# PEER's first products from slab 44 on: three 256-column products a chunk instead of one of 512 and one of 256, with no fold on VectorE

## The chip, the cores and the metric

One Trainium2 chip, one of its cores. The metric is the device time of one execution in microseconds (us), as the median of several runs. The kernel before takes 2194.0 us (three runs, 2193.04 to 2195.11).

## The reference

A small transformer over 256 tokens of width 1024, in float32: an MLA attention layer, a PEER layer, a GLA layer, a second PEER layer, and then a block with two kinds of local attention and a gated FFN. The change lies in PEER, which is run twice:

```python
def one_block(xi):
    q = (xi @ w_query).reshape(B, T, PEER_HEADS, 2, PEER_HALF)
    s = jnp.einsum('bthcd,cnd->bthcn', q, sub_keys)
    s_top, i_top = lax.top_k(s, PEER_TOPK)
    cand = s_top[..., 0, :, None] + s_top[..., 1, None, :]
    ...
    gate = jax.nn.softmax(best, axis=-1)
    u = u_tab[idx]
    h = jax.nn.gelu(jnp.einsum('bthkd,btd->bthk', u, xi), approximate=False)
    w = (gate * h)
    return jnp.einsum('bthk,bthkd->btd', w, v_tab[idx])
```

The kernel gathers nothing. It multiplies all 16384 rows of u (128 slabs of 128 experts) with all tokens, takes Gelu of everything, multiplies with a gate that is zero for the experts that were not chosen, and multiplies the result with all of v. So each PEER layer is two dense products of 256 x 1024 x 16384.

## The kernel before, in words

**Products in parts.** Every float32 weight and every activation is split into a high part (rounded to the type that TensorE multiplies in one pass, fp32r) and a low part, the rest. A product is then the sum of three: high weight x high activation, high weight x low activation, low weight x high activation.

**The slab stream.** Weights come in slabs of 128 x 1024 float32 (512 KB), in one order fixed for the whole kernel. SyncE loads slab n into `raw` (4 buffers, L237). ScalarE writes the high part `hi` (`split_hi`, L250) once the products of slab n-3 have been made (semaphore `eaten`; `hi` and `lo` have 3 buffers, `RING`). GpSimd or VectorE writes `lo` (`split_lo`, L259). TensorE waits for `hi_done`, does the products with `hi`, waits for the low part, does those with `lo`, and raises `eaten`. A slab's parts stand in buffers of 1088 columns, and the pair (a, b) at the end of `add_slab` says how many columns in the high and the low part begin: `SKEW` is 16 columns, which is 64 bytes.

**The activations** `xx` are 8 chunks (c) of 128 rows x 512 columns: 256 columns of the high part `xh`, then 256 of the low part `xl`.

**First products of PEER** (`first(i)`, i = 0 to 127, u). In slabs 0 to 43 each chunk c takes three products of 256 columns: `hi` with `xh` (L1434), `hi` with `xl` (L1435) and `lo` with `xh` (L1439), 24 a slab, all added up in the same 256 columns of bank i % 3. From slab 44 (`LEAD`) on, `hi` is the stationary operand of one product of 512 columns over `xh` and `xl` together (L1428, seven a slab, and the eighth in L1442 after the low ones), and `lo` that of one of 256 columns (L1439, eight a slab). The high-high and high-low sums then stand beside one another in the bank, and VectorE adds them up (`fold`, L1712, into `whole`) before ScalarE takes Gelu (L1562, L1564).

**What else runs from slab 44 on.** Until then VectorE finds the chosen experts. After that, in 64 of 84 slabs, a group of 4 tokens is turned into gates: VectorE writes one-hot rows (L1700, L1702, L1704), ScalarE their low parts (L1581), TensorE makes eight small f16 products behind the slab's own (`sums`, L1467), and VectorE multiplies the gates in (`gate_slab` L1720, `apply` L1728). The pattern repeats every five slabs: four with a group behind them, one without.

**Second products** (`second(v)`, v): the activations are stationary and the slab moves, twelve products of 512 columns each (L1480, L1481, L1487). They need `pe_ml`, which VectorE writes (L1734).

Every engine works through its own fixed list of instructions; nothing is reordered while the kernel runs.

Of the kernel before, what the change touches and what calls it, by code (L numbers as in the profile page):

```python
# [8 lines left out]
ALU = mybir.AluOpType  # L9
ACT = mybir.ActivationFunctionType  # L10
AX_X = mybir.AxisListType.X
# [6 lines left out]
P = 128  # L18
D = 1024
KD = D // P  # L20
T = 256
# [14 lines left out]
H_P, NK, TOPK = 8, 128, 16  # L36
# [64 lines left out]
SKEW, SLOT = 16, 1088  # L101
# [50 lines left out]
def add_slab(k, src, x, e, low, skew=(0, 0)):  # L152

    k.lows[low] += 1
    k.slabs.append((src, x, e, skew))
    k.lo_at.append((low, k.lows[low]))


def weight_stream(k):
# [16 lines left out]
    for l in range(2):  # L176
        w = k.dram[f"w_query{l}"]
        for c in range(2):
            for b in range(4):
                add_slab(k, rows_of(w, 2 * b, 2, c * 512, 512), 2, 512, k.lo_dve, (SKEW, SKEW))  # L180
        for i in range(NK):
            add_slab(k, k.dram["peer_u"][l, i], KD, P, k.lo_pool, (0 if i >= LEAD else SKEW, SKEW))
        for i in range(NK):
            add_slab(k, k.dram["peer_v"][l, i].unsqueeze(1), 1, D, k.lo_dve)
        if l == 0:
            w = k.dram["gla_w_in"]
            for c0 in (G_Q, G_LOW, G_K, G_V, G_V + 512, G_R, G_R + 512):
                if c0 == G_LOW:
                    add_slab(k, rows_of(w, 0, KD, c0, R_G), KD, R_G, k.lo_dve)
                else:  # L190
                    for b in range(4):
                        add_slab(k, rows_of(w, 2 * b, 2, c0, 512), 2, 512, k.lo_dve,
                                 (SKEW, SKEW) if c0 in (G_Q, G_K) else (0, 0))
            out_slabs(k, k.dram["gla_w_o"])
# [1084 lines left out]
TURN, LEAD = 41, 44  # L1279
# [23 lines left out]
def peer(k, l, s0, norm, after):  # L1303
# [3 lines left out]
    first_part = k.sig("bd_first_part")  # L1307
    G = NT * H_P
    names = ("q_act", "q_dve", "zeroed", "keyed", "scored", "s_act", "s_dve", "counted", "raised", "powered",
             "ranked", "turned", "equal", "hotted", "lowered", "summed", "spread", "applied", "bent", "gated", "m_hi", "m_lo", "folded")  # L1310
    (q_act, q_dve, zeroed, keyed, scored, s_act, s_dve, counted, raised, powered, ranked, turned, equal, hotted,
     lowered, summed, spread, applied, bent, gated, m_hi, m_lo, folded) = (k.sig(f"pe_{x}") for x in names)
    hi, lo = k.hi, k.lo
    u0, v0, end = s0 + U0, s0 + V0, s0 + SLABS
    with ExitStack() as ctx:
        hidden = k.sb(ctx, "pe_hidden", [P, NK, T])
# [5 lines left out]
        mh = k.sb(ctx, "pe_mh", [P, 2, T], F32R)  # L1322
        ml = k.sb(ctx, "pe_ml", [P, 2, T], F32R)
        count = k.sb(ctx, "pe_count", [P, NK], I32)
        whole = k.sb(ctx, "pe_whole", [P, 2, T])

# [39 lines left out]
        with k.nc.Block() as block:  # L1368
# [11 lines left out]
            def _(pe):  # L1380
# [33 lines left out]
                def first(i):  # L1414

                    r = (u0 + i) % RING
                    if i >= 3:

                        j = i - 3
                        if j > LEAD:  # L1420
                            pe.wait_ge(gated.sem, gated_before(j))
                        else:
                            pe.wait_ge(bent.sem, bent.at(j + 1))
                    ps = first_ps(i)
                    pe.wait_ge(k.hi_done, u0 + i + 1)
                    if i >= LEAD:
                        for c in range(KD - 1):
                            pe.matmul(k.bank[i % 3][:], hi[:, r, c * P:(c + 1) * P],  # L1428
                                      k.xx[:, c].rearrange("p s t -> p (s t)"), start=(c == 0), stop=False,
                                      skip_group_check=True)  # L1430
                    else:
                        for c in range(KD):
                            cols = slice(SKEW + c * P, SKEW + (c + 1) * P)
                            pe.matmul(ps, hi[:, r, cols], k.xh[:, c], start=(c == 0), stop=False)  # L1434
                            pe.matmul(ps, hi[:, r, cols], k.xl[:, c], start=False, stop=False)  # L1435
                    pe.wait_ge(*k.lo_at[u0 + i])
                    for c in range(KD):
                        cols = slice(SKEW + c * P, SKEW + (c + 1) * P)
                        last = pe.matmul(ps, lo[:, r, cols], k.xh[:, c], start=False,  # L1439
                                         stop=(c == KD - 1 and i < LEAD), skip_group_check=(i >= LEAD))  # L1440
                    if i >= LEAD:
                        last = pe.matmul(k.bank[i % 3][:], hi[:, r, (KD - 1) * P:KD * P],  # L1442
                                         k.xx[:, KD - 1].rearrange("p s t -> p (s t)"), start=False, stop=True,
                                         skip_group_check=True)
                    last.then_inc(k.eaten, 1)

                def turn_slots():
# [91 lines left out]
            def _(act):  # L1539
# [12 lines left out]
                def bend(i):  # L1552

                    g = grouped(i)
                    if i >= LEAD:
                        act.wait_ge(folded.sem, folded.at(i - LEAD + 1))
                    else:
                        act.wait_ge(k.eaten, u0 + i + 1)
                    ps, cut = first_ps(i), g * GROUP
                    made = whole[:, i % 2] if i >= LEAD else ps  # L1560
                    if cut:
                        last = act.activation(ps[:, 0:cut], made[:, 0:cut], ACT.Gelu)  # L1562
                    if cut < T:
                        last = act.activation(hidden[:, i, cut:], made[:, cut:], ACT.Gelu)  # L1564
                    last.then_inc(bent.sem, 1)

                def keep_sums(g):
# [30 lines left out]
                for n in range(SLABS):  # L1598
# [13 lines left out]
                    i = n - U0  # L1612
# [19 lines left out]
            def _(dve):  # L1632
# [71 lines left out]
                    dve.tensor_tensor(hot_h[:, g % 2], hot_ps(g)[:].rearrange("p (t i) -> p t i", t=GROUP), over(2, g),  # L1704
                                      ALU.mult).then_inc(hotted.sem, 1)

                def fold(i):

                    dve.wait_ge(k.eaten, u0 + i + 1)
                    if i >= LEAD + 2:  # L1710
                        dve.wait_ge(bent.sem, bent.at(i - 1))
                    dve.tensor_reduce(whole[:, i % 2], k.bank[i % 3][:].rearrange("p (s t) -> p t s", s=2), AX_X, ALU.add)\  # L1712
                       .then_inc(folded.sem, 1)

                def gate_slab(i):

                    cut = grouped(i) * GROUP
# [32 lines left out]
                one_hots(0)  # L1750
                one_hots(1)
                for i in range(LEAD, NK):
                    fold(i)
                    g = GROUP_AT.get(i)
                    if g is not None and g + 2 < GROUPS:
                        one_hots(g + 2)
                    if i > LEAD:
                        gate_slab(i)
                    if g is not None:
                        apply(g)  # L1760
                    if i >= NK - 3:
                        split_lo(k, dve, u0 + i + RING)
                    if i >= NK - 2:
                        split_middle(i - NK + 2)
# [14 lines left out]
    for x in (bent, m_hi, m_lo):  # L1779
        x.advance(NK)  # L1780
    gated.advance(NK - LEAD - 1)
    folded.advance(NK - LEAD)
    for x in (equal, hotted, lowered, summed, spread, applied):
        x.advance(GROUPS)
    for x in (zeroed, counted, raised, powered, ranked, turned):
# [1370 lines left out]
```

## Time and profile before

| | |
|---|---|
| median of three runs | 2194.0 us |
| span of the profiled execution, first to last instruction | 2186.9 us |
| TensorE busy | 2151.9 us (98%) |
| VectorE, ScalarE, GpSimd busy | 1561.2, 1249.5, 709.9 us |
| mean granted TensorE clock | 0.996 of full speed |
| slabs 44 to 127, layer 1 | 288.85 to 555.87 us |
| slabs 44 to 127, layer 2 | 1180.34 to about 1447.4 us |

The profile gives no time of its own for the profiled execution beside the span; the median of the runs is 7.1 us above it. Matmul records overlap (a product's record is longer than the distance to the next), so the pace of TensorE is read from the distance between starts, not from durations. A few records are missing from the trace, so counts can be a few short.

### The profile page before, as it was taken

How to read it: one execution, taken by the hardware profiler on the slowest of the kernel's cores; microseconds unless marked ns; L12 is line 12 of the kernel's file. 1: busy time of each engine (PE TensorE's matmuls, PEld its weight loads, DVE VectorE, ACT ScalarE, POOL GpSimd, SP SyncE). 2: the span in 40 equal slices, each digit the busy share in tenths (PEclk: the TensorE clock that was granted, in tenths of full speed). 3: DMA queues.
4: the chain of work that ended last, by engine and by line, in shares of the span. 5: the costliest groups of instructions: out<-in, count | busy, mean ns of one | idle time of the engine just before them, and what ended most of it. 6: DMA issues, size and time to landing. Idle time of an engine off the chain costs nothing. (4 is left out here: it accounts for less than half of the span.)

```text
span 2186.9 us, 35587 instructions
## 1 busy us (share of the span) xinstructions
PE 2151.9 (98%) x13179; PEld 1877.7 (86%) x13179; DVE 1561.2 (71%) x2946; ACT 1249.5 (57%) x2471; POOL 709.9 (32%) x346
## 2 busy tenths in 40 slices
PE   8899999999999999999999999999999999999999
PEld 8789998888888888887999888888888888897888
DVE  8658978888666666666698788866666669457776
ACT  6544577777455555564446777755555555555443
POOL 3217977777000000001698777730000005100000
PEclk9999999999999999999999999999999999999999
DMA  5244655555555555553555554556666656435554
GB/s 166 65 147 155 203 174 164 164 165 166 190 193 193 193 194 195 167 166 108 174 192 184 166 164 164 165 183 192 193 193 193 194 171 228 129 113 164 189 192 153
DMA packets 122956, 375.34 MB, mean 172 GB/s; under 512 B 13200, under 2 KB 18064, under 8 KB 122784
## 3 DMA queue, kind: packets, MB, share of 16 engines
q1 hardware_dynamic: 122496, 373.05, 52.7%
q8 instruction: 106, 1.74, 0.3%
q14 instruction: 66, 0.54, 0.1%
q10 hardware_dynamic: 288, 0.01, 0.0%
HBM read 371.96 MB, written 1.05 MB: 171 GB/s over the span
## 5 line engine op out<-in xcount | busy, mean ns | idle before, releaser
L250 ACT ACTIVATE hi<-raw 128x1024 fp32r<-128x1024 f32 (+2 forms) x705 | 738.3, 1048 | 359.9 <-PE bank L1439 109.7
L259 DVE TENSOR_TENSOR lo<-raw,hi 128x1024 fp32r<-128x1024 f32 (+2 forms) x447 | 542.1, 1216 | 263.3 <-ACT hi L250 262.8
L259 POOL TENSOR_TENSOR lo<-raw,hi 128x1024 fp32r<-128x1024 f32 x258 | 626.2, 2431 | 229.1 <-ACT hi L250 228.7
L1480 PE MATMUL bank<-hi,pe_mh 128*128 128x512 f32 x1016 | 395.7, 389 | 1.3 <-DVE pe_ml L1734 1.3
L1481 PE MATMUL bank<-hi,pe_ml 128*128 128x512 f32 x1016 | 395.3, 389 | 0.0
L1428 PE MATMUL bank<-xx,hi 128*128 128x512 f32 x1176 | 308.9, 401 | 0.0
L1593 ACT ACTIVATE pe_mh<-pe_hidden 128x256 fp32r<-128x256 f32 x256 | 106.9, 418 | 342.0 <-PE bank L1487 342.0
L342 POOL TENSOR_TENSOR rstd<-mean,minus_half 128x2 f32<-128x2 f32 x6 | 4.2, 704 | 898.9 <-DVE mean L335 898.9
L1439 PEld LDWEIGHTS bank<-xx,lo 128*128 128x128 f32 x2048 | 269.4, 188 | 13.9
L1439 PE MATMUL bank<-xx,lo 128*128 128x256 f32 x2048 | 280.5, 280 | 0.0
L1487 PE MATMUL bank<-lo,pe_mh 128*128 128x512 f32 x1016 | 271.6, 389 | 0.0
L1428 PEld LDWEIGHTS bank<-xx,hi 128*128 128x128 f32 x1176 | 211.2, 188 | 37.8
L1480 PEld LDWEIGHTS bank<-hi,pe_mh 128*128 128x128 f32 x1016 | 190.7, 188 | 42.1 <-DVE pe_ml L1734 2.6
L1487 PEld LDWEIGHTS bank<-lo,pe_mh 128*128 128x128 f32 x1016 | 190.7, 188 | 39.7
L1481 PEld LDWEIGHTS bank<-hi,pe_ml 128*128 128x128 f32 x1016 | 190.7, 188 | 39.4
L1734 DVE TENSOR_TENSOR pe_ml<-pe_hidden,pe_mh 128x256 fp32r<-128x256 f32 x256 | 108.9, 426 | 137.9 <-ACT pe_mh L1593 137.9
L1581 ACT ACTIVATE pe_hot_l<-bank,pe_slots 128x128 f16<-128x128 f32 x512 | 145.8, 369 | 80.3 <-DVE pe_hot_h L1704 80.3
L1434 PE MATMUL bank<-xx,hi 128*128 128x256 f32 x704 | 167.3, 279 | 0.0
L1435 PE MATMUL bank<-xx,hi 128*128 128x256 f32 x704 | 166.3, 278 | 0.0
L1712 DVE TENSOR_REDUCE pe_whole<-bank 128x256 f32<-128x512 f32 x168 | 116.2, 692 | 59.0 <-PE bank L1442 56.5
L1434 PEld LDWEIGHTS bank<-xx,hi 128*128 128x128 f32 x704 | 132.6, 188 | 0.1
L1435 PEld LDWEIGHTS bank<-xx,hi 128*128 128x128 f32 x704 | 132.5, 188 | 0.1
(418 smaller groups left out, 3405.5 us busy)
## 6 DMA issues: line engine op xcount, KB each, us to landing
raw<-in_peer_u SPq DMA_DIRECT2D x256, 512.0 KB, 3.3
raw<-in_peer_v SPq DMA_DIRECT2D x256, 512.0 KB, 3.5
raw<-in_w_gate_up SPq DMA_DIRECT2D x44, 512.0 KB, 3.5
raw<-in_w_in SPq DMA_DIRECT2D x34, 512.0 KB, 4.2
raw<-in_gla_w_in SPq DMA_DIRECT2D x24, 512.0 KB, 3.6
raw<-in_w_down SPq DMA_DIRECT2D x22, 512.0 KB, 3.3
raw<-in_w_query SPq DMA_DIRECT2D x16, 512.0 KB, 3.3
raw<-in_mla_w_o SPq DMA_DIRECT2D x8, 512.0 KB, 3.3
```

Of the source, the lines that this page charges most:

```text
L250: act.activation(k.hi[:, n % RING, at_hi:at_hi + x * e], k.raw[:, n % RAW, 0:x * e], ACT.Copy).then_inc(k.hi_done, 1)
L259: eng.tensor_tensor(k.lo[:, n % RING, at_lo:at_lo + x * e], k.raw[:, n % RAW, 0:x * e], k.hi[:, n % RING, at_hi:at_hi + x * e].bitcast(F32 ...
L1428: pe.matmul(k.bank[i % 3][:], hi[:, r, c * P:(c + 1) * P], k.xx[:, c].rearrange("p s t -> p (s t)"), start=(c == 0), stop=False, skip_grou ...
L1434: pe.matmul(ps, hi[:, r, cols], k.xh[:, c], start=(c == 0), stop=False)
L1435: pe.matmul(ps, hi[:, r, cols], k.xl[:, c], start=False, stop=False)
L1439: last = pe.matmul(ps, lo[:, r, cols], k.xh[:, c], start=False, stop=(c == KD - 1 and i < LEAD), skip_group_check=(i >= LEAD))
L1480: pe.matmul(second_ps(a, c), mh[:, v % 2, tok], hi[:, r, half], start=(v == 0), stop=False)
L1481: pe.matmul(second_ps(a, c), ml[:, v % 2, tok], hi[:, r, half], start=False, stop=False)
L1487: last = pe.matmul(second_ps(a, c), mh[:, v % 2, tok], lo[:, r, half], start=False, stop=(v == NK - 1))
L1581: last = act.activation(hot_l[:, g % 2, t], hot_ps(g)[:, t * NK:(t + 1) * NK], ACT.Copy, scale=slots[:, 3, c:c + 1])
L1712: dve.tensor_reduce(whole[:, i % 2], k.bank[i % 3][:].rearrange("p (s t) -> p t s", s=2), AX_X, ALU.add)\
L1734: dve.tensor_tensor(ml[:, v % 2], hidden[:, v], mh[:, v % 2].bitcast(F32), ALU.subtract)\
```

## The change

`first(i)` makes the 24 products of 256 columns in all 128 slabs. The high part stands 16 columns off in all of them, as the low part does already. All sums go into the bank's first 256 columns, ScalarE takes Gelu from there, and waits for `eaten` instead of for the fold. `fold`, its semaphore and its buffer are gone.

```diff
-            add_slab(k, k.dram["peer_u"][l, i], KD, P, k.lo_pool, (0 if i >= LEAD else SKEW, SKEW))
+            add_slab(k, k.dram["peer_u"][l, i], KD, P, k.lo_pool, (SKEW, SKEW))
...
                     pe.wait_ge(k.hi_done, u0 + i + 1)
-                    if i >= LEAD:
-                        for c in range(KD - 1):
-                            pe.matmul(k.bank[i % 3][:], hi[:, r, c * P:(c + 1) * P],
-                                      k.xx[:, c].rearrange("p s t -> p (s t)"), start=(c == 0), stop=False,
-                                      skip_group_check=True)
-                    else:
-                        for c in range(KD):
-                            cols = slice(SKEW + c * P, SKEW + (c + 1) * P)
-                            pe.matmul(ps, hi[:, r, cols], k.xh[:, c], start=(c == 0), stop=False)
-                            pe.matmul(ps, hi[:, r, cols], k.xl[:, c], start=False, stop=False)
+                    for c in range(KD):
+                        cols = slice(SKEW + c * P, SKEW + (c + 1) * P)
+                        pe.matmul(ps, hi[:, r, cols], k.xh[:, c], start=(c == 0), stop=False)
+                        pe.matmul(ps, hi[:, r, cols], k.xl[:, c], start=False, stop=False)
                     pe.wait_ge(*k.lo_at[u0 + i])
...
-                    if i >= LEAD:
-                        last = pe.matmul(k.bank[i % 3][:], hi[:, r, (KD - 1) * P:KD * P],
-                                         k.xx[:, KD - 1].rearrange("p s t -> p (s t)"), start=False, stop=True,
-                                         skip_group_check=True)
                     last.then_inc(k.eaten, 1)
...
-                    if i >= LEAD:
-                        act.wait_ge(folded.sem, folded.at(i - LEAD + 1))
-                    else:
-                        act.wait_ge(k.eaten, u0 + i + 1)
+                    act.wait_ge(k.eaten, u0 + i + 1)
                     ps, cut = first_ps(i), g * GROUP
-                    made = whole[:, i % 2] if i >= LEAD else ps
...
-                def fold(i):
-
-                    dve.wait_ge(k.eaten, u0 + i + 1)
-                    if i >= LEAD + 2:
-                        dve.wait_ge(bent.sem, bent.at(i - 1))
-                    dve.tensor_reduce(whole[:, i % 2], k.bank[i % 3][:].rearrange("p (s t) -> p t s", s=2), AX_X, ALU.add)\
-                       .then_inc(folded.sem, 1)
...
                 for i in range(LEAD, NK):
-                    fold(i)
```

TensorE (PE), before, slab 45 and the beginning of the group behind it; `bank<-xx,hi` is a product with a high part, `pe_hot` are the one-hot rows:

```order
L1428 MATMUL bank<-xx,hi 128x512 [waits hi_done,pe_bent]
L1428 MATMUL bank<-xx,hi 128x512 x6
L1439 MATMUL bank<-xx,lo 128x256 [waits lo_pool]
L1439 MATMUL bank<-xx,lo 128x256 x7
L1442 MATMUL bank<-xx,hi 128x512
L1467 MATMUL bank<-pe_hot_h,pe_hot_j 128x128 [waits pe_lowered,pe_hotted]
L1467 MATMUL bank<-pe_hot_l,pe_hot_j 128x128
```

TensorE after the change, the end of a slab's sixteen high products and the same group (the lines have moved up: L1427 and L1428 are now the two high products of 256 columns, L1432 the low one, L1455 the group's):

```order
L1427 MATMUL bank<-xx,hi 128x256
L1428 MATMUL bank<-xx,hi 128x256
L1432 MATMUL bank<-xx,lo 128x256 [waits lo_pool]
L1432 MATMUL bank<-xx,lo 128x256 x7
L1455 MATMUL bank<-pe_hot_h,pe_hot_j 128x128 [waits pe_lowered,pe_hotted]
L1455 MATMUL bank<-pe_hot_l,pe_hot_j 128x128
```

Eight products of 512 columns have become sixteen of 256, none of them behind the low ones any more; the group and all waits of TensorE stand where they stood.

VectorE (DVE), before, what it does for slab 46 up to the fold of slab 47:

```order
L1712 TENSOR_REDUCE pe_whole<-bank 128x256 [waits pe_bent,eaten]
L1700 TENSOR_TENSOR bank<-bank,pe_slots 128x512 [waits pe_summed,pe_lowered]
L1702 TENSOR_TENSOR pe_hot_j<-bank,pe_slots 128x512
L1704 TENSOR_TENSOR pe_hot_h<-bank,pe_slots 128x512 [waits pe_equal]
L1720 TENSOR_TENSOR pe_hidden<-pe_hidden,bank 128x8 [waits pe_spread,pe_bent]
L1728 SCALAR_TENSOR_TENSOR pe_hidden<-bank,pe_hidden 128x47x4 [waits pe_spread,pe_bent]
L1712 TENSOR_REDUCE pe_whole<-bank 128x256 [waits pe_bent,eaten]
```

VectorE after the change, the same slab (L1684, L1686, L1688 are the one-hot rows, L1696 and L1704 the gates):

```order
L1684 TENSOR_TENSOR bank<-bank,pe_slots 128x512 [waits pe_summed,pe_lowered]
L1686 TENSOR_TENSOR pe_hot_j<-bank,pe_slots 128x512
L1688 TENSOR_TENSOR pe_hot_h<-bank,pe_slots 128x512 [waits pe_equal]
L1696 TENSOR_TENSOR pe_hidden<-pe_hidden,bank 128x8 [waits pe_spread,pe_bent]
L1704 SCALAR_TENSOR_TENSOR pe_hidden<-bank,pe_hidden 128x47x4 [waits pe_spread,pe_bent]
```

Only the fold has gone; the rest stands in the same order.

VectorE before, where the first products end and the second begin (slabs 126 and 127; `pe_ml` is what the second products wait for):

```order
L1712 TENSOR_REDUCE pe_whole<-bank 128x256 [waits pe_bent,eaten]
L1720 TENSOR_TENSOR pe_hidden<-pe_hidden,bank 128x256 [waits pe_spread,pe_bent]
L259 TENSOR_TENSOR lo<-raw,hi 128x1024 [waits hi_done]
L1734 TENSOR_TENSOR pe_ml<-pe_hidden,pe_mh 128x256 [waits pe_m_hi]
L1712 TENSOR_REDUCE pe_whole<-bank 128x256 [waits pe_bent,eaten]
L1720 TENSOR_TENSOR pe_hidden<-pe_hidden,bank 128x256 [waits pe_spread,pe_bent]
L259 TENSOR_TENSOR lo<-raw,hi 128x1024 [waits hi_done]
L1734 TENSOR_TENSOR pe_ml<-pe_hidden,pe_mh 128x256 [waits pe_m_hi] x2
```

After the change, the same place (L1710 writes `pe_ml`):

```order
L1696 TENSOR_TENSOR pe_hidden<-pe_hidden,bank 128x256 [waits pe_spread,pe_bent]
L259 TENSOR_TENSOR lo<-raw,hi 128x1024 [waits hi_done]
L1710 TENSOR_TENSOR pe_ml<-pe_hidden,pe_mh 128x256 [waits pe_m_hi]
L1696 TENSOR_TENSOR pe_hidden<-pe_hidden,bank 128x256 [waits pe_spread,pe_bent]
L259 TENSOR_TENSOR lo<-raw,hi 128x1024 [waits hi_done]
L1710 TENSOR_TENSOR pe_ml<-pe_hidden,pe_mh 128x256 [waits pe_m_hi] x2
```

Here too only the fold of each slab has gone.

## Rows read from the trace of the kernel before

**Rows 1.** Page, part 1: engine busy us (share of span) xinstructions.

```profile
PE 2151.9 (98%) x13179; PEld 1877.7 (86%) x13179; DVE 1561.2 (71%) x2946; ACT 1249.5 (57%) x2471; POOL 709.9 (32%) x346
```

**Rows 2.** Waits, 292 to 540 us: engine line waited for: total us, times, longest.

```profile
ACT pe_hot_l L1581 <- DVE pe_hot_h L1704: 40.1, 62, 0.9
DVE pe_whole L1712 <- PE bank L1442: 24.9, 53, 1.1
ACT hi L250 <- PE bank L1442: 17.2, 15, 1.2
PEld bank L1467 <- issue: 9.9, 62, 0.2
```

**Rows 3.** Timeline, PE, slabs from 44 on: start us, us, engine line op xcount.

```profile
400.81 1.77 PE L1428 MATMUL bank<-xx,hi 128*128 128x512 f32 x7
402.41 1.11 PE L1439 MATMUL bank<-xx,lo 128*128 128x256 f32 x8
403.36 0.40 PE L1442 MATMUL bank<-xx,hi 128*128 128x512 f32 x1
403.60 0.23 PE L1467 MATMUL bank<-pe_hot_h,pe_hot_j 128*128 128x128 f16 x1
...
404.02 1.86 PE L1428 MATMUL bank<-xx,hi 128*128 128x512 f32 x7
405.72 1.09 PE L1439 MATMUL bank<-xx,lo 128*128 128x256 f32 x8
...
416.80 1.09 PE L1428 MATMUL bank<-xx,hi 128*128 128x512 f32 x4
```

**Rows 4.** Timeline, PE, low products of slabs 26 and 28.

```profile
241.02 1.07 PE L1439 MATMUL bank<-xx,lo 128*128 128x256 f32 x8
...
246.46 1.07 PE L1439 MATMUL bank<-xx,lo 128*128 128x256 f32 x8
```

**Rows 5.** Timeline, PE, low products of slabs 5 and 8.

```profile
182.35 1.11 PE L1439 MATMUL bank<-xx,lo 128*128 128x256 f32 x8
...
190.83 1.11 PE L1439 MATMUL bank<-xx,lo 128*128 128x256 f32 x8
```

**Rows 6.** Timeline, PE, second products, the last four of two slabs three apart.

```profile
599.67 1.07 PE L1487 MATMUL bank<-lo,pe_mh 128*128 128x512 f32 x4
...
607.83 1.07 PE L1487 MATMUL bank<-lo,pe_mh 128*128 128x512 f32 x4
```

**Rows 7.** Timeline, PE, slab 42, which follows on six transposes.

```profile
283.31 0.37 PE L1434 MATMUL bank<-xx,hi 128*128 128x256 f32 x1
...
285.22 1.07 PE L1439 MATMUL bank<-xx,lo 128*128 128x256 f32 x8
```

**Rows 8.** Timeline, PE, second block's low products: first and last of 15 slabs.

```profile
1870.20 1.07 PE L2432 MATMUL bank<-xx,lo 128*128 128x256 f32 x8
...
1942.75 1.10 PE L2432 MATMUL bank<-xx,lo 128*128 128x256 f32 x8
```

**Rows 9.** Page, part 5: the fold.

```profile
L1712 DVE TENSOR_REDUCE pe_whole<-bank 128x256 f32<-128x512 f32 x168 | 116.2, 692 | 59.0 <-PE bank L1442 56.5
```

**Rows 10.** Timeline, all engines, slab 127 and first two slabs of second products.

```profile
553.09 1.77 PE L1428 MATMUL bank<-xx,hi 128*128 128x512 f32 x7
553.35 1.06 ACT L250 ACTIVATE hi<-raw 128x1024 fp32r<-128x1024 f32 x1 [1.45 <-PE bank L1442]
...
554.71 0.42 DVE L1720 TENSOR_TENSOR pe_hidden<-pe_hidden,bank 128x256 f32<-128x256 f32 x1 [0.62 <-ACT bank L1562]
555.05 1.22 DVE L259 TENSOR_TENSOR lo<-raw,hi 128x1024 fp32r<-128x1024 f32 x1
...
556.18 0.42 DVE L1734 TENSOR_TENSOR pe_ml<-pe_hidden,pe_mh 128x256 fp32r<-128x256 f32 x1
556.52 0.68 DVE L1712 TENSOR_REDUCE pe_whole<-bank 128x256 f32<-128x512 f32 x1
556.66 0.19 PEld L1480 LDWEIGHTS bank<-hi,pe_mh 128*128 128x128 f32 x1 [0.95 <-DVE pe_ml L1734]
...
559.61 0.50 PE L1480 MATMUL bank<-hi,pe_mh 128*128 128x512 f32 x1
```

More of the change, by code:

```diff
@@ L1309, in peer @@
     names = ("q_act", "q_dve", "zeroed", "keyed", "scored", "s_act", "s_dve", "counted", "raised", "powered",
-             "ranked", "turned", "equal", "hotted", "lowered", "summed", "spread", "applied", "bent", "gated", "m_hi", "m_lo", "folded")
+             "ranked", "turned", "equal", "hotted", "lowered", "summed", "spread", "applied", "bent", "gated", "m_hi", "m_lo")
     (q_act, q_dve, zeroed, keyed, scored, s_act, s_dve, counted, raised, powered, ranked, turned, equal, hotted,
-     lowered, summed, spread, applied, bent, gated, m_hi, m_lo, folded) = (k.sig(f"pe_{x}") for x in names)
+     lowered, summed, spread, applied, bent, gated, m_hi, m_lo) = (k.sig(f"pe_{x}") for x in names)
     hi, lo = k.hi, k.lo
@@ L1324, in peer @@
         count = k.sb(ctx, "pe_count", [P, NK], I32)
-        whole = k.sb(ctx, "pe_whole", [P, 2, T])
         spare = Carver(hidden[:, NK // 2:, :].rearrange("p i t -> p (i t)"))
@@ L1438, in first @@
                         cols = slice(SKEW + c * P, SKEW + (c + 1) * P)
-                        last = pe.matmul(ps, lo[:, r, cols], k.xh[:, c], start=False,
-                                         stop=(c == KD - 1 and i < LEAD), skip_group_check=(i >= LEAD))
-                    if i >= LEAD:
-                        last = pe.matmul(k.bank[i % 3][:], hi[:, r, (KD - 1) * P:KD * P],
-                                         k.xx[:, KD - 1].rearrange("p s t -> p (s t)"), start=False, stop=True,
-                                         skip_group_check=True)
+                        last = pe.matmul(ps, lo[:, r, cols], k.xh[:, c], start=False, stop=(c == KD - 1))
                     last.then_inc(k.eaten, 1)
@@ L1554, in bend @@
                     g = grouped(i)
-                    if i >= LEAD:
-                        act.wait_ge(folded.sem, folded.at(i - LEAD + 1))
-                    else:
-                        act.wait_ge(k.eaten, u0 + i + 1)
+                    act.wait_ge(k.eaten, u0 + i + 1)
                     ps, cut = first_ps(i), g * GROUP
-                    made = whole[:, i % 2] if i >= LEAD else ps
                     if cut:
-                        last = act.activation(ps[:, 0:cut], made[:, 0:cut], ACT.Gelu)
+                        last = act.activation(ps[:, 0:cut], ps[:, 0:cut], ACT.Gelu)
                     if cut < T:
-                        last = act.activation(hidden[:, i, cut:], made[:, cut:], ACT.Gelu)
+                        last = act.activation(hidden[:, i, cut:], ps[:, cut:], ACT.Gelu)
                     last.then_inc(bent.sem, 1)
@@ L1781, in peer @@
     gated.advance(NK - LEAD - 1)
-    folded.advance(NK - LEAD)
     for x in (equal, hotted, lowered, summed, spread, applied):
```

## The prediction

> **What bounds the kernel now.** First the busy shares of the page: TensorE is busy for 98% of the span, the next engine for 71% [rows 1]. So the time is TensorE's, unless it waits. The waits of the stretch that the change touches (292 to 540 us, nearly all of slabs 44 to 127 of the first PEER layer) come next: VectorE, ScalarE and GpSimd wait there for TensorE or for one another, and TensorE for nobody; the one entry of its own is 9.9 us on the weight-load side in front of the groups' products, put down to issue [rows 2]. In 252 us TensorE gains nothing from any other engine being faster. What a slab costs there is the distance between the starts of its products, and that is what the timeline of TensorE is for.
>
> From the start of one slab that has no group in front of it to the next such slab, five slabs and four groups later, it is 416.80 - 400.81 = 15.99 us [rows 3]. A group takes from 403.60 to about 404.03, 0.43 us, so five slabs cost 15.99 - 4 x 0.43 = 14.27 us. The slab without a group in front: 400.81 to 403.60, 2.79 us. The other four: (14.27 - 2.79) / 4 = 2.87 us each. They are dearer by 0.08 to 0.09 us because the first product after the small f16 products starts late: the seven high products last 1.86 us against 1.77 [rows 3].
>
> **What three products of 256 columns cost.** The same 24 products are in this trace, in slabs 0 to 43, with both parts 64 bytes off. They run at two paces. Slabs 26 to 28: low products start at 241.02 and, two slabs later, at 246.46, so 2.72 us a slab, 113.3 ns a product [rows 4]. Slabs 5 to 8: 182.35 to 190.83, three slabs, 2.827 us a slab, 117.8 ns a product [rows 5]. I call them fast and slow; nothing waits in either, and eight low products last 1.07 us in the fast one and 1.10 to 1.11 in the slow one, which is how a pace is recognised at a glance. The columns, the places and the types are the same; the clock is full in both. So the operations alone do not decide the cost.
>
> Is there a fixed price for sixteen products instead of eight? The second products, twelve of 512 columns a slab, take (607.83 - 599.67) / 3 = 2.72 us [rows 6], the same as 24 of 256 columns at the fast pace [rows 4]: 226.7 ns against twice 113.3. I take zero. The Trainium skill ("TensorE: Matmul & The Clock Gate", section on the back-to-back issue gap) gives N / 2.4 + 2.5 ns a product, which speaks against this change: eight more products a slab would be 8 x 2.5 = 20 ns, over 168 slabs 3.4 us more. By these rows it isn't so: here each pace is 17/16 of the columns for both widths. The sum goes by the rows.
>
> Now the old form against the new, by slab. The first product after a group keeps its delay, for it comes from the change of kind in front of it: after the six transposes slab 42 needs 285.22 - 283.31 = 1.91 us for its sixteen high products, 16 x 0.1133 = 1.81 and 0.09 to 0.10 for the start [rows 7]. So:
> - fast: 2.72 + 0.09 = 2.81 after a group (before: 2.87, gain 0.06), 2.72 otherwise (before: 2.79, gain 0.07);
> - slow: 2.83 + 0.09 = 2.92 after a group (loss 0.05), 2.83 otherwise (loss 0.04).
>
> A layer has 64 slabs with a group behind them, so 64 that follow on one, and 20 others; the last of these doesn't count, because what comes after it waits for VectorE (below). All fast: 64 x 0.06 + 19 x 0.07 = 5.2 us gained a layer, 10.3 in both. All slow: 64 x 0.05 + 19 x 0.04 = 4.0 us lost, 7.9 in both. These are the bounds of the one term that matters.
>
> **Which value in between.** A pace, once taken, is kept while slabs follow on one another (5 to 8, 26 to 28), and it is taken anew after other products have come between. In the second block 256-column slabs of the same kind are broken up by small attention products just as these will be by groups: of 15 such slabs 7 are fast and 8 slow, and the marks alternate more than they cluster (the first is 1.07, the last 1.10) [rows 8]. Slab 42, after transposes, is fast [rows 7]. The old form itself shows a mark of the same kind: its eight low products last 1.11 us in the slab without a group and 1.09 in the one after [rows 3]. Nothing in the trace has f16 products of 128 columns directly in front of 256-column ones, so I take half of the slabs at either pace: -1.2 us over both layers, halfway between -10.3 and +7.9.
>
> The Trainium skill (same page, "Step-by-step: what each phase is for") says that TensorE has two independent read ports, and that loading the next weights doesn't steal from the running product. By that the slow pace would have no ground and all slabs would be fast. The trace has both paces; that sentence is the case for the first rival.
>
> **Edits of no cost.** The fold is 116.2 us of VectorE's time, 692 ns each [rows 9], and it is hidden: nobody on TensorE's side waits for it between the first and the last slabs [rows 2]. Without it the one-hot rows and the gates come earlier, ScalarE takes Gelu from the bank as it does in slabs 0 to 43, and these engines wait longer for TensorE instead. The bank of a slab comes free for the third slab after it, some 8 us later; a later Gelu could not be felt either. The high part at another offset costs ScalarE nothing that I can see a reason for; ScalarE waits for TensorE there anyway [rows 2]. DMA issues are the same and hang on the same low parts.
>
> **Where the fold does stand on the path: the switch to the second products.** TensorE's first one waits for `pe_ml`. That chain starts when slab 126's u part is needed no more, at 553.09: ScalarE's high part first (553.35), Gelu, then VectorE's gate 554.71, low part 555.05, `pe_ml` 556.18, and TensorE starts at 556.66, 3.57 us after 553.09 [rows 10]. The fold isn't in it: the gate waits for ScalarE, which was held by the high part [rows 10]. So this stays at 3.57 us, and a shorter slab 127 just waits longer; hence the slab that I leave out. The next one is different: after `pe_ml` comes the fold of slab 127, 556.52 for 0.68 us, and the gate, low part and second `pe_ml` behind it; the second V slab starts 559.61 - 556.66 = 2.95 us after the first, where the pace is 2.72 [rows 6, 10]. Without the fold I expect that 0.23 back, and a little behind it: 0.3 us a layer, 0.6 in all. Bounds: nothing, and 0.7 a layer.
>
> **Sum.** -1.2 - 0.6 = -1.8 us. The profiled span of 2186.9 us would become 2185.1; the median lies 7.1 us above that span, so 2192.2 us.
>
> **Rivals.**
> - *Nearly all slabs fast.* For it: slab 42 [rows 7], and slabs 26 to 28, which stay fast [rows 4]. Against it: 8 of 15 in rows 8. Gain 10.3 + 0.6: 2183.1 us.
> - *Nearly all slabs slow*, the one on the other side. The place is the first product after each group; the price is 24 x 4.5 ns = 0.11 us a slab above the fast pace. It decides from the point where more than about 85% of the slabs are slow, since at 57% the old form is reached (0.06 of 0.11). For it: slabs 5 to 8 stay slow though nothing disturbs them [rows 5]; the group repeats on a fixed beat, so all may fall the same way. Loss 7.9 - 0.6: 2201.3 us.
> - *The change takes the pressure off VectorE and that is the gain.* Then ScalarE's 40.1 us of waiting for the one-hot rows [rows 2] would have to reach TensorE. They don't; it would give the 0.6 us at the switch alone, 2193.4 us, inside the forecast.
>
> **How the numbers follow.** This kernel's runs lie within about 0.1% of one another, and 0.2% (4.4 us) is about what can be told from no change: the bounds are 2189.6 and 2198.4 us. Below the first the share of fast slabs must be over about two thirds, above the second under about one seventh. Mixed paces, the forecast, 0.39, with its own range 2189.6 to 2196; nearly all fast 0.37, because the two places closest in kind, in PEER itself and behind a short run of 128-column products, are both fast [rows 4, 7]; nearly all slow 0.24. Faster 0.37, same 0.39, slower 0.24. The range that leaves out a tenth at either side: 2183.0 to 2200.5.
>
> **What would show it.** In the profile after: the rows of eight low products, 1.07 (fast) or 1.10 to 1.11 (slow), counted over the 168 slabs, with 2.81 or 2.92 us from the first product after a group to the next group; 2.72 or 2.83 in the slabs without; a mixture of both is my forecast, one alone a rival. The first second product 3.57 us after slab 127 begins, the next one 2.7 to 2.8 later. No new wait of TensorE between. The forecast is wrong if TensorE waits for Gelu or for the groups, if the first product after a group is late by another amount than 0.09 us, or if a third pace turns up.

## The result, and the profile after

| | before | after |
|---|---|---|
| median of eight runs each | 2193.52 us (2190.14 to 2195.85) | 2199.06 us (2196.97 to 2204.24) |
| ratio after / before | | 1.0028, interval 1.0019 to 1.0038 |
| span of the profiled execution | 2186.9 us | 2196.5 us |
| slab 44 to slab 127, first product to first product, layer 1 | 264.24 us | 267.60 us |
| the same, layer 2 | 264.24 us | 267.50 us |

The change makes the kernel slower, by 0.28%. The forecast was 2192.2 us, a gain of 1.8; the loss of 5.5 us lies near the second rival (2201.3 us, nearly all slabs slow). The two profiled spans lie 9.6 us apart, which overstates it: the run profiled after took 2198.19 us, 1.7 above its span, while the median before lies 6.6 above the profiled span, so by the same 1.7 a quick execution was profiled there. The two stretches account for 3.3 us a layer, 6.6 in all. Of the rest 2.6 us arise from slab 127 of layer 1 to slab 44 of layer 2, nearly all of it code that the change doesn't touch, and eight executions of the changed kernel differ by 7.3 us among themselves; I draw nothing from that part. The medians and ratios below leave out two executions far off all others, one of e8 (5373 us) and one of e10 (3584 us).

The page after, part 1, answers to [rows 1]; VectorE is 104 us less busy, TensorE 10 us more.

```profile
PE 2161.8 (98%) x14523; PEld 1954.8 (89%) x14523; DVE 1457.6 (66%) x2778; ACT 1243.2 (57%) x2471; POOL 709.2 (32%) x346
```

The waits from 292 to 540 us answer to [rows 2]:

```profile
POOL lo L259 <- ACT hi L250: 65.2, 78, 1.0
DVE bank L1684 <- PE bank L1455: 63.5, 62, 1.6
ACT pe_hot_l L1565 <- DVE pe_hot_h L1688: 42.7, 61, 0.9
DVE pe_hidden L1696 <- ACT pe_hidden L1548: 28.7, 15, 2.2
ACT hi L250 <- PE bank L1432: 19.9, 15, 1.3
```

TensorE still waits for nobody in this stretch. VectorE waits more for TensorE, 63.5 us here in front of the one-hot rows, where it waited 24.9 in front of the fold [rows 2]. No wait explains the loss, so the pace must.

Timeline of TensorE after, slabs 44 to 46 (the first row of each slab after a group is its late first product) and, as "x8", each slab's low products:

```profile
291.06 1.07 PE L1432 MATMUL bank<-xx,lo 128*128 128x256 f32 x8
292.01 0.22 PE L1455 MATMUL bank<-pe_hot_h,pe_hot_j 128*128 128x128 f16 x1
...
292.43 0.36 PE L1427 MATMUL bank<-xx,hi 128*128 128x256 f32 x1
...
294.40 1.10 PE L1432 MATMUL bank<-xx,lo 128*128 128x256 f32 x8
295.34 0.23 PE L1455 MATMUL bank<-pe_hot_h,pe_hot_j 128*128 128x128 f16 x1
...
295.77 0.36 PE L1427 MATMUL bank<-xx,hi 128*128 128x256 f32 x1
...
297.74 1.10 PE L1432 MATMUL bank<-xx,lo 128*128 128x256 f32 x8
```

Slab 44 comes fast out of slabs 26 to 43. Behind the first group the mark goes from 1.07 to 1.10, and a slab lasts 295.34 - 292.43 = 2.91 us, the slow figure of the forecast (2.92). It stays so. Of the 64 slabs behind a group all are slow in layer 1 and 63 in layer 2, where only the slab behind the first group is still fast; of the 20 others 19 are slow in either layer, all but slab 44. The five-slab beat, which was 15.99 us [rows 3], is now 321.57 - 305.37 = 16.20 us:

```profile
305.37 0.28 PE L1427 MATMUL bank<-xx,hi 128*128 128x256 f32 x1
...
308.20 0.23 PE L1455 MATMUL bank<-pe_hot_h,pe_hot_j 128*128 128x128 f16 x1
...
321.57 0.28 PE L1427 MATMUL bank<-xx,hi 128*128 128x256 f32 x1
```

16.6 such beats make 3.5 us a layer. The switch to the second products answers to [rows 10] (all engines after; slab 127 begins at 556.85):

```profile
557.11 1.06 ACT L250 ACTIVATE hi<-raw 128x1024 fp32r<-128x1024 f32 x1 [1.49 <-PE bank L1432]
...
558.47 0.42 DVE L1696 TENSOR_TENSOR pe_hidden<-pe_hidden,bank 128x256 f32<-128x256 f32 x1 [1.27 <-ACT bank L1546]
558.73 1.10 PE L1432 MATMUL bank<-xx,lo 128*128 128x256 f32 x8
558.81 1.22 DVE L259 TENSOR_TENSOR lo<-raw,hi 128x1024 fp32r<-128x1024 f32 x1
...
559.95 0.42 DVE L1710 TENSOR_TENSOR pe_ml<-pe_hidden,pe_mh 128x256 fp32r<-128x256 f32 x1
560.42 0.50 PE L1468 MATMUL bank<-hi,pe_mh 128*128 128x512 f32 x1 [0.58 <-DVE pe_ml L1710]
...
563.27 0.47 PE L1468 MATMUL bank<-hi,pe_mh 128*128 128x512 f32 x1
```

The first second product comes 3.57 us after slab 127 begins, as before; the next one 2.85 us later (before: 2.95).

### The profile page after: what moved, and what is told of

Same layout as the page of the kernel before. It is cut to its first block and busy times, and to the rows that moved or that the text cites. A ratio compares the mean times of both kernels' runs of the same rounds, so it can differ in the third digit from the quotient of the medians.

```text
span 2196.5 us, 37943 instructions
## 1 busy us (share of the span) xinstructions
PE 2161.8 (98%) x14523; PEld 1954.8 (89%) x14523; DVE 1457.6 (66%) x2778; ACT 1243.2 (57%) x2471; POOL 709.2 (32%) x346
## 5 line engine op out<-in xcount | busy, mean ns | idle before, releaser
L1427 PE MATMUL bank<-xx,hi 128*128 128x256 f32 x2048 | 502.0, 286 | 0.0
L1428 PE MATMUL bank<-xx,hi 128*128 128x256 f32 x2048 | 490.3, 280 | 0.0
L1428 PEld LDWEIGHTS bank<-xx,hi 128*128 128x128 f32 x2048 | 387.6, 189 | 0.1
L1427 PEld LDWEIGHTS bank<-xx,hi 128*128 128x128 f32 x2048 | 386.9, 189 | 0.1
L1432 PE MATMUL bank<-xx,lo 128*128 128x256 f32 x2048 | 281.2, 280 | 0.0
L1432 PEld LDWEIGHTS bank<-xx,lo 128*128 128x128 f32 x2048 | 257.6, 189 | 0.2
L1710 DVE TENSOR_TENSOR pe_ml<-pe_hidden,pe_mh 128x256 fp32r<-128x256 f32 x256 | 109.1, 426 | 137.8 <-ACT pe_mh L1577 137.8
L1684 DVE TENSOR_TENSOR bank<-bank,pe_slots 128x512 f32<-128x512 f32 x128 | 89.5, 700 | 126.9 <-PE bank L1455 126.8
L1696 DVE TENSOR_TENSOR pe_hidden<-pe_hidden,bank 128x256 f32<-128x256 f32 (+47 forms) x166 | 47.9, 288 | 83.7 <-ACT pe_hidden L1548 65.2
L1688 DVE TENSOR_TENSOR pe_hot_h<-bank,pe_slots 128x512 f16<-128x512 f32 x128 | 87.2, 681 | 0.0
```

The lines of the kernel that those rows point to most:

```text
L1684: dve.tensor_tensor(hot_ps(g)[:].rearrange("p (t i) -> p t i", t=GROUP), each, over(0, g), ALU.is_equal).then_inc(equal.sem, 1)
L1710: dve.tensor_tensor(ml[:, v % 2], hidden[:, v], mh[:, v % 2].bitcast(F32), ALU.subtract)\
```

## The experiments

A break is what stands between two slabs on TensorE, here the group's small products; a bubble is a moment in which TensorE stands idle. Ratios are to the kernel before, run beside it, with 95% intervals. Where one execution was made, its profiled span stands; the changed kernel's is 2196.5 us. The edits are shortened. e1 and e12 to e14 leave products of the groups out, so their gates are wrong: e1 all of them, e12, e13 and e14 those of three, two and one of a group's four tokens.

**Is it the break, or the load of VectorE and ScalarE?** The slow pace sets in together with the groups, but the groups bring work for all engines.

e1_no_groups, on the kernel after (the same in `sums` in all kernels of this kind):

```diff
-                    for t in range(GROUP):
-                        for hot in (hot_h, hot_l):
-                            last = pe.matmul(group_ps(g)[...], ...)
-                    last.then_inc(summed.sem, 1)
+                    pe.nop().then_inc(summed.sem, 1)
```

> The changed kernel with the eight f16 products behind 64 slabs of each layer left out (TensorE only raises the semaphore; the gates are garbage), so slabs 44 to 127 follow on one another. Theory 'the pace is set anew at each break and then kept': slab 43 is fast, so all 84 stay fast, 2.72 us a slab, x8 rows of 1.07; the span falls by 64 x (0.43 + 0.09) x 2 = 66.6 us for the groups and their late first products and by 168 x 0.107 = 18 us for the pace, to about 2112. Rival 'VectorE's and ScalarE's load on SBUF in this stretch slows TensorE': the one-hot rows are still written, so 2.83 us a slab, x8 rows of 1.10, span about 2130.

Measured: span 2110.4 us, all slabs fast (2.72 us, but for one of 2.88 and one of 2.82 a layer at the first would-be group). Timeline of TensorE, two slabs after each other behind the first would-be group:

```profile
293.65 1.07 PE L1432 MATMUL bank<-xx,lo 128*128 128x256 f32 x8
...
296.37 1.07 PE L1432 MATMUL bank<-xx,lo 128*128 128x256 f32 x8
```

The other engines' work was all there: VectorE was busy for 1463.1 us and ScalarE for 1243.6, against 1457.6 and 1243.2 in the kernel after. So the slow pace comes with the small products, not with the load.

e2_f32_after_group, on the kernel after: one small float32 product ahead of each slab behind a group.

```diff
+                    if i - 1 in GROUP_AT:
+                        pe.matmul(k.bank[i % 3][:, T:T + P], k.ident[:], k.ident[:], start=True, stop=True)
```

> The changed kernel with one float32 product of 128 columns (identity by identity, into the unused half of the slab's own bank) put between a group's f16 products and the slab behind it. Theory 'the kind of the last product in a break sets the pace': behind six float32 transposes slab 42 was fast, so the slabs behind a group become fast (x8 rows 1.07): 168 x 0.107 = 18 us less for the pace, about 0.11 to 0.22 us x 128 = 14 to 28 us more for the extra products. Rival 'any break does it, and the place in the beat decides': still 1.10, or a mixture.

Measured: span 2227.3 us; slow (2.91 us) but for the first slab (2.83). A float32 product as the last one before the slab doesn't make it fast. The break is also about 0.24 us longer here, so this run says nothing of the kind at equal length.

**Is it where the operands lie?** The numbers are where the high and the low part begin, in columns of 4 bytes, from slab 44 on; the products read from the same place.

```diff
-            add_slab(k, k.dram["peer_u"][l, i], KD, P, k.lo_pool, (SKEW, SKEW))
+e3          add_slab(k, ..., k.lo_pool, (0 if i >= LEAD else SKEW, SKEW))
+e4          add_slab(k, ..., k.lo_pool, (32 if i >= LEAD else SKEW, 32 if i >= LEAD else SKEW))
+e6 (on the kernel before, whose high part began at 0)    add_slab(k, ..., k.lo_pool, (SKEW, SKEW))
```

> The changed kernel with the high part of slabs 44 to 127 at no offset and the low part 64 bytes off, as before the change, products as after it. Theory 'break': offsets don't matter, every slab behind a group slow as in the changed kernel, span 2196.5 within 1 us. Theory 'the place of stationary and moving operand in SBUF decides': the 16 high products, which alone are moved, run at another pace than the low ones: 1.81 or over 1.97 us for 16 of them, the low ones unchanged at 0.94.

> The changed kernel with both parts of slabs 44 to 127 128 bytes off instead of 64. Theory 'break': no change, span 2196.5 within 1 us, x8 rows 1.10. Theory 'place': another pace in all 24 products; if fast, 2.72 and 2.82 us a slab and 18 us less, about 2179.

> The kernel before with one part of the change alone: the high part of slabs 44 to 127 64 bytes off, still one product of 512 columns a chunk and the fold. Theory 'only three products of 256 columns are sensitive, for there the weight loads follow most closely': same as before within 1 us. Rival 'offsets matter to the 512 form too' (e3 showed 0.03 us a slab for the 256 form): 0.03 us x 168 = 5 us, in either direction.

Measured: e3 span 2201.3 us, 2.94 us a slab behind a group and 2.86 to 2.87 elsewhere; e4 2197.6 us, 2.93 and 2.84 to 2.85; e6, timed, 0.9996 (0.9984 to 1.0008). The place is worth 0.01 to 0.04 us a slab in the new form. In the old form the timing shows nothing of it, and in the profiled executions a layer's stretch takes 263.6 us (e6) against 264.2. Both parts 64 bytes off is the best of the three, and still slow. So the 64 bytes are not at fault.

**Fewer breaks, or a bubble in them.** The groups two at a time (e7 on the kernel after, e8 on the one before), so that 32 breaks of 16 products replace 64 of 8:

```diff
-                    if i in GROUP_AT:
-                        sums(GROUP_AT[i])
+                    if i in GROUP_AT and GROUP_AT[i] % 2:
+                        sums(GROUP_AT[i] - 1)
+                        sums(GROUP_AT[i])
```

In e5 (on the kernel after) TensorE waits for the end of its own group, in e11 only behind every fourth; e9 (on the kernel before) puts such a wait behind the score products, ahead of slab 2; e10 is e8 and e9 together.

```diff
                     last.then_inc(summed.sem, 1)
+e5                  pe.wait_ge(summed.sem, summed.at(g + 1))
+e11                 if g % 4 == 3: pe.wait_ge(summed.sem, summed.at(g + 1))
...
                 for h in range(4, H_P):
                     scores(h)
+e9, e10         pe.wait_ge(scored.sem, scored.at(H_P))
```

> The changed kernel in which TensorE waits, behind each group, for the end of the group's own last product, so that it stands idle for a moment before the next slab. Theory 'bubble': what sets the slow pace is that a product of one kind runs straight into one of another; after a moment of idleness the pace is fast (as in e1, behind the bare semaphore operation, and at 219 us of the kernel before, where a stall ended the slow pace). Then x8 rows 1.07 and 24 products in 2.72 to 2.82 us; the idleness costs 0.25 to 0.35 us x 128 = 32 to 45 us, the pace gives 18 back: about 2211 to 2224. Rival 'every break makes it slow': x8 rows 1.10 and 2229 to 2242.

> The changed kernel with the groups' products two groups at a time, behind every second slab that had one: 32 breaks a layer instead of 64. Theory 'break': all slabs slow (2.83), but half of the late starts of 0.09 us go: 64 x 0.09 = 5.8 us less than the changed kernel, about 2193.5. If the pace also falls back to fast within a longer row of slabs, up to 18 us more. Rival: VectorE or ScalarE becomes late because the one-hot buffers come free a slab later, and TensorE waits: slower than the changed kernel.

> The kernel before with the groups' products two groups at a time: 32 breaks a layer instead of 64. Theory 'break': 64 late starts of 0.09 us fewer, 5.8 us less than before, ratio 0.997. Rival: the fold and the one-hot rows on VectorE are late because buffers come free a slab later, TensorE waits, no gain or a loss.

> The kernel before with one wait more in each layer: behind the last score products (before slab 2) TensorE waits for their end. Theory 'bubble': slabs 2 to 17 of both layers, slow in every run so far (2.83 us), become fast (2.72): 16 x 0.107 = 1.7 us a layer less, 0.3 us for the idleness and 0.2 more or less at slab 18, where the stall at 219 us goes or moves: about 3 us less in all, ratio 0.9987. Rival 'slabs 2 to 17 are slow because of what VectorE does there (the top-16 search)': pace stays 2.83, time 0.6 us more.

> Both of what helped or should help, on the old form: groups in pairs (e8) and the wait behind the scores (e9). By the sum of both: 5.8 + 3 = 9 us less than before, ratio 0.996; by what e8 measured (0.9988) and e9's forecast, 0.9975.

> The changed kernel with the wait of e5 behind every fourth group only, so that one break in four has a bubble. It asks what a break does to a fast pace. Theory 'a break without a bubble always makes it slow': the slab behind the bubble and the one directly behind it fast (x8 rows 1.07), the three behind the next groups slow (1.10). Rival 'a break keeps the pace that was there, and only the first one tips it by chance' (in layer 2 of the changed kernel the slab behind the first group was still fast, the next slow): more than two of five fast. Time: 32 bubbles of 0.29 us = 9 us more, 64 fast slabs x 0.107 = 7 less, 2198 against 2196.5 of span.

e5: span 2217.3 us. Its rows of TensorE, one slab and the group behind it:

```profile
291.74 0.39 PE L1427 MATMUL bank<-xx,hi 128*128 128x256 f32 x1
...
293.68 1.07 PE L1432 MATMUL bank<-xx,lo 128*128 128x256 f32 x8
294.59 0.23 PE L1455 MATMUL bank<-pe_hot_h,pe_hot_j 128*128 128x128 f16 x1
...
295.27 0.39 PE L1427 MATMUL bank<-xx,hi 128*128 128x256 f32 x1
```

All slabs are fast (mark 1.07, 2.85 us with a first product that is 0.12 late), but a break now takes (295.27 - 291.74) - 2.72 = 0.81 us beyond the fast slab, where it took (295.77 - 292.43) - 2.83 = 0.51 beyond the slow one: the bubble costs more than the pace gives. This bore out the idea written down ahead of it, that a slab is fast behind a moment of idleness. e9 seemed to do so too: slabs 2 to 17 ran at 2.72 us instead of 2.83. e11 ended it. Its rows around the fourth group, whose bubble lies before 301.23:

```profile
296.26 1.10 PE L1432 MATMUL bank<-xx,lo 128*128 128x256 f32 x8
...
301.23 0.39 PE L1427 MATMUL bank<-xx,hi 128*128 128x256 f32 x1
...
303.22 1.10 PE L1432 MATMUL bank<-xx,lo 128*128 128x256 f32 x8
```

The same late start (0.39) and the same bubble as in e5, and the slab behind it is slow, 1.99 us of high products: span 2205.6 us, all slow but the first. A bubble alone doesn't make a slab fast. In e5 the slabs ahead of each bubble are fast, in e11 they are slow, and both stay as they were.

e7, timed, 1.0013 (1.0002 to 1.0024): slow (2.91 and 2.83 us), with 64 late starts fewer. e8 0.9988 (0.9977 to 0.9999): the old form with the same saving, which by 64 late starts of 0.09 us would be 5.8 us. Its trace has 262.0 us a layer from slab 44 to 127 against 264.24, so 4.5 of them; the medians differ by 2.8, and by the interval anything from 0.2 to 5.0 is possible. e9 0.9998 (0.9987 to 1.0008) though its slabs were fast as expected. Of 16 x 0.11 = 1.8 us a layer 0.8 went at slab 18 and 0.4 in the wait that was added (slab 1 to slab 2 took 6.69 us instead of 6.29); the 0.6 that stayed are too little for the timing to show. Timelines of e9, of TensorE, then GpSimd, then VectorE:

```profile
219.75 1.18 PE L1439 MATMUL bank<-xx,lo 128*128 128x256 f32 x8 [0.73 <-POOL lo L259]
```

```profile
210.28 2.40 POOL L259 TENSOR_TENSOR lo<-raw,hi 128x1024 fp32r<-128x1024 f32 x1 [0.32 <-ACT hi L250]
213.00 6.69 POOL L259 TENSOR_TENSOR lo<-raw,hi 128x1024 fp32r<-128x1024 f32 x1 [0.32 <-ACT hi L250]
```

```profile
213.02 4.42 DVE L1666 TENSOR_TENSOR pe_hidden<-pe_hidden 128x4096 f32<-128x4096 f32 x1
```

The low part that begins beside VectorE's one long tensor-tensor takes 6.69 us instead of 2.40, and slab 18 lasts 3.72 us, where it lasted 2.95 in the kernel before. The same is there in the kernel before, GpSimd:

```profile
212.96 6.12 POOL L259 TENSOR_TENSOR lo<-raw,hi 128x1024 fp32r<-128x1024 f32 x1 [0.43 <-ACT hi L250]
```

TensorE had arrived earlier only to wait longer. e10, timed, 0.9982 (0.9971 to 0.9992).

**The length of the break.** What e5 and e11 left was the timing of the break itself. So its count of small products was varied, each worth about 55.5 ns, everything else as in the kernel after.

```diff
-                    for t in range(GROUP):
+e12                 for t in range(1):
+e13                 for t in range(2):
+e14                 for t in range(3):
+e16                 for t in (0, 0, 1, 2, 3):
```

> The changed kernel with only two of the eight products of each group (the gates of three tokens in four are then garbage). It asks whether the length of the break matters. Theory 'running straight from one kind into the other does it': slow behind each, 128 x 6 x 0.055 = 42 us less than the changed kernel, span about 2154, x8 rows 1.10. Rival 'a break must be long enough': fast (1.07), 18 us less again, about 2136.

> The changed kernel with four of the eight products of each group (the gates of two tokens in four are then garbage). By length alone the pace turns once between 2 (fast) and 8 (slow) products. If fast: 128 x 4 x 0.055 = 28 us and 18 us less than the changed kernel's 2196.5 of span, 2150; if slow 2168. Theory 'exact time of the start': either, and not in order of length over the three runs.

> The same with six of eight (one token in four garbage). If fast 2196.5 - 14 - 18 = 2164, if slow 2182. By length: slow if the run with four is slow. By exact time: either.

> The changed kernel with ten products behind each slab that has a group (the first token's two are made twice, so nothing is left out). By length: slow, 2196.5 + 14 = 2211 of span. By exact time: possibly fast, 2193.

| products in a break | 2 (e12) | 4 (e13) | 6 (e14) | 8 (after) | 10 (e16) |
|---|---|---|---|---|---|
| span, us | 2140.0 | 2167.9 | 2182.8 | 2196.5 | 2192.1 |
| a slab behind it, us | 2.82 to 2.83 | 2.91 | 2.91 to 2.92 | 2.91 | 2.82 to 2.83 |
| pace | fast from the third slab on | slow | slow | slow | fast from the third slab on |

In e12 and e16 the first two slabs behind groups are slow; then all are fast. In e13 and e14 the first one is fast; then all are slow. So each length has a pace into which the loop settles. Timeline of TensorE in e16:

```profile
292.98 1.10 PE L1432 MATMUL bank<-xx,lo 128*128 128x256 f32 x8
...
296.43 1.10 PE L1432 MATMUL bank<-xx,lo 128*128 128x256 f32 x8
...
297.92 0.37 PE L1427 MATMUL bank<-xx,hi 128*128 128x256 f32 x1
...
299.84 1.07 PE L1432 MATMUL bank<-xx,lo 128*128 128x256 f32 x8
```

e16 does more work than the kernel after and is quicker: from the low products of slab 44 to those of slab 127 it takes 556.88 - 289.53 = 267.35 us, against 558.73 - 291.06 = 267.67, with 64 x 0.11 = 7.0 us of added small products in it. Of the 4.4 us between the two spans these stretches give only 0.3 in layer 1 and as much in layer 2; the rest lies outside them and isn't the pace.

e15_group_mid_slab, on the kernel after, moves the same eight products into the slab that they stood behind, between its high and its low products:

```diff
+                    if i in GROUP_AT:
+                        sums(GROUP_AT[i])
                     pe.wait_ge(*k.lo_at[u0 + i])
...
-                    if i in GROUP_AT:
-                        sums(GROUP_AT[i])
```

> The changed kernel with the group's eight products between the high and the low products of its slab instead of behind it. The late start of 0.09 us stays, since a float32 part follows on f16 again. By length: slow, the same as the changed kernel within 1 us, ratio 1.003 to before. By exact time, or by the place of the operands that follow (low parts instead of high): it may be fast, 18 us less than the changed kernel, ratio 0.995.

Measured 1.0042 (1.0030 to 1.0055), slow; a layer's stretch takes 268.5 us, 0.9 more than in the kernel after, which was not followed up. With eight products another place within the slab doesn't give the fast pace.

**The length at two groups a break.** If 16 is slow like 8, and 10 fast like 2, then 18 should be fast and 20 slow. On e7:

```diff
-                    for t in range(GROUP):
+e17                 for t in ((0, 1, 2, 3) if g % 2 else (0, 0, 1, 2, 3)):
+e18                 for t in (0, 0, 1, 2, 3):
```

> The changed kernel with the groups in pairs (e7) and two products made twice in each pair, so 18 products in a break. Theory 'the pace repeats with every eighth product of the break': fast, so 18 us less than e7 for the pace and 64 x 2 x 0.055 = 7 us more for the products: span 2189.1 - 11 = 2178, ratio to before about 0.996, faster than both kernels. Rival 'no such rule': slow, 2196.

> The same with four made twice, 20 products in a break. Same theory: slow, span 2189.1 + 14 = 2203, x8 rows 1.10. Rival: fast, 2185.

Measured: e18 span 2205.4 us, slow; e17 0.9961 (0.9949 to 0.9974), 2183.85 us against 2191.20 for the kernel before, so better than both kernels, with the reference's whole work in it. Two slabs of e17 behind a pair of groups:

```profile
295.50 0.37 PE L1427 MATMUL bank<-xx,hi 128*128 128x256 f32 x1
...
297.41 1.07 PE L1432 MATMUL bank<-xx,lo 128*128 128x256 f32 x8
...
300.13 1.07 PE L1432 MATMUL bank<-xx,lo 128*128 128x256 f32 x8
...
302.03 0.37 PE L1427 MATMUL bank<-xx,hi 128*128 128x256 f32 x1
```

A break is what 302.03 - 300.13 = 1.90 us leave beside eight low products of 0.91 us together, so 0.99 us. The pattern sums to what the trace shows: 83 x 2.72 us, and 32 breaks of 0.99 us with 0.10 for the late start behind each, is 260.6 us from slab 44 to 127; the timeline has 551.63 - 290.88 = 260.75. The kernel before takes 264.24.

## Why the prediction was wrong

- **What bounds the kernel: right.** TensorE waited for nobody in the stretch, before or after (it is 248 us long, not 252). Taking 104 us of work off VectorE gave nothing but 0.2 us at the switch.
- **Each pace: right.** 2.91 us behind a group and 2.83 without (forecast 2.92 and 2.83), and in e17 2.82 and 2.72 (forecast 2.81 and 2.72). The late first product is there (0.36 instead of 0.28 us, the slab 0.08 to 0.10 longer). Sixteen products have no price of their own beside eight: 24 of 256 columns in 2.72 us, like twelve of 512. That "each pace is 17/16 of the columns" holds for the fast one alone; for the slow one, 117.8 ns, it doesn't.
- **"I take half of the slabs at either pace": this step failed.** Nearly every slab was slow: 127 of the 128 behind a group. Instead of -1.2 us the term was +6.6, near its bound of +7.9. With the 0.2 us gained at the switch that makes 6.4; the medians differ by 5.5, with an interval of about 4.2 to 8.3. The count in rows 8 was taken as odds for each slab by itself. But the pace is no draw: in e12 to e18 the loop settles within three groups into one pace; which one it is goes with the length of the break, and that is the same at all 64 groups. The text of the second rival had this ("the group repeats on a fixed beat, so all may fall the same way") and the forecast didn't use it. With "all alike" as the reading, what stays is mainly a choice between -10.3 and +7.9.
- **The evidence for fast was no evidence.** Slab 42 stands behind transposes and the attention products have other lengths; e12 to e18 show that two small products more or less can turn the pace. Nothing that was read in the trace of before told which way eight would fall; that it came out slow is not explained by any step of the forecast.
- **The switch: right in place, less than half in size.** 3.57 us stayed; the second slab gave back 0.10 us a layer and not 0.23. What is left is the chain itself: gate, low part and `pe_ml` follow on one another from 561.30 to about 563.2.
- **The rule of the two read ports.** By the Trainium skill ("TensorE: Matmul & The Clock Gate", "Step-by-step: what each phase is for") loading the next weights takes no reading bandwidth from the running product; the prediction read this as the case for all slabs fast. The trace after has the slow pace all the same: 16.20 us a beat with no wait in it, of which 16.20 - 4 x 0.43 - 4 x 0.09 - 5 x 2.72 = 0.5 us is the slow pace. Whether the weight loads have a part in it no run here shows, so the reading failed and the rule itself was not tested. The gap rule of the Trainium skill (same page, "Back-to-back issue gap"; N / 2.4 + 2.5 ns, so 109.2 ns at 256 columns), which the page itself calls that of the isolated product, fits neither 113.3 nor 117.8 ns.

**What stays open.** Why the length goes with the pace. Breaks of 2, 10 and 18 products of about 55.5 ns end up fast, and of 4, 6, 8, 16 and 20 slow, which looks like a period of eight products (444 ns), but odd counts were not tried, nor 12 and 14, and no break at all (e1) leaves the pace fast where 8 and 16 products don't. Most of the lengths rest on one execution each, with the same pace in both layers; 8, 16 and 18 were timed several times. The length isn't all: eight products turned the pace at the first group in layer 1 and at the second in layer 2, and e5 and e11 share one bubble and differ in pace, so the state in which TensorE enters a break counts as well. Whether it is the length, the count or the exact time of the next start that acts was not told apart, and the mechanism inside the engine was not shown.

## What to carry to other kernels

Where the same operations appear at two paces in a trace and the cause isn't known, don't average them: ask what sets the pace and whether that thing repeats, since a loop can put all its turns on one side. A short interruption of a long run of products costs something behind it as well: here a break of 0.43 us, then 0.09 for the late start and 0.11 a slab for the slow pace. Its length is worth trying by one or two dummy products (e17: two products, 0.11 us, added to each break and the breaks halved in number, 0.39% gained over the kernel before). And an engine that the bounding engine doesn't wait for gives nothing when it is relieved.

## What the hardware showed unexpectedly

- 256-column products of fp32r, each with its own weights, run at 113.3 or 117.8 ns with the granted clock at 1.00 in both (kernel before, 241 to 247 us and 182 to 191 us), and keep the pace until something interrupts them: in the kernel before, slabs 2 to 17 are slow, slab 18 is held up by 0.1 us, and slabs 19 to 43 are fast.
- Where the stationary operand begins matters slightly at the slow pace: a slab that doesn't follow on a group takes 2.83 us with both parts at 64 bytes, 2.84 to 2.85 with both at 128 (e4), and 2.86 to 2.87 with the high part at 0 and the low at 64 (e3).
- A low part of GpSimd that ran beside a VectorE tensor-tensor of 128x4096 took 6.12 us in the kernel before and 6.69 in e9, instead of 2.40.
